# Stick-breaking attention layer: mask added at the scores, projections and output split into quarters and pairs between the head pairs

## The chip, the cores and the metric

One core of a Trainium2 chip runs the whole program, a stack of six stages in float32. The metric is the device time of one execution in microseconds. A core has five engines with an instruction stream each: TensorE (PE, matmuls into the accumulation memory PSUM), VectorE (DVE), ScalarE (ACT), GpSimd (POOL), and SyncE (SP), which here only issues transfers. They synchronize through semaphores.

## The reference, cut to what matters

The program computes conv mixer, experts, stick-breaking attention, experts, a state-space and dilated attention layer, and block attention, on 256 tokens of width 1024, with layer or RMS norms between. The change is in the third stage:

```python
z = jnp.einsum("bhqd,bhkd->bhqk", qb, kb) * scale
causal = s_idx < t_idx
log_keep = jnp.where(causal, jax.nn.log_sigmoid(-z), 0.0)
later = lax.cumsum(log_keep, axis=3, reverse=True) - log_keep
a = jnp.where(causal, jnp.exp(jax.nn.log_sigmoid(z) + later), 0.0)
outs.append(jnp.einsum("bhqk,bhkd->bhqd", a.astype(vb.dtype), vb))
...
return jnp.einsum("bse,ed->bsd", o, w_o)
```

16 heads of 64 columns; `x = layer_norm(ALPHA * x + mix)` follows. The expert stage behind it routes every token to 2 of 32 experts, and the kernel streams the weights of all 32.

## The kernel before, in words

Activations lie on 128 partitions, in two tiles of 128 tokens (`x[:, t]`), and transposed (`xT`). Weights come in chunks of 2 MB through a ring of six slots: SP's `load(g)` waits until chunk g - 6 has been used (`chunk_done`), then fills its slot. The stick-breaking stage has 8 chunks: q, k, v for heads 0 to 7 (chunks 0, 1, 2), the same for heads 8 to 15 (3, 4, 5), and the output matrix in two halves (6, 7). The first four-expert group of the next stage also loads four chunks outside the ring; the first of them waits until all chunks of the stage before are used (`sp.wait_ge(chunk_done, b0)`, L430). After that the expert weights stream without a stop.

PE's order in the stage (`stick_breaking`, L852 on): transposes of x, projection chunks 0 and 1 (`channels`, L587) and 2 (`tokens`, L597) whole, then ten turns of a loop over pairs of heads. Turn n issues `z(n+1)`, the transposed scores of pair n+1 (banks 0 and 1, 384 columns for each head, that is three 128x128 blocks); `fill()`, a half of projection chunk 3, 4 or 5 (L873, L878; eight or sixteen matmuls into bank 6 or 7) in the first five turns, two in turn 0; `later(n-1)`, the running sums over keys as matmuls with a triangular and an all-ones matrix (banks 2 and 3, L904 to L908); and `mix(n-2)`, weights times values (bank 4 or 5, L922, L925). In turns 8 and 9 the output of chunk 6 stands before `later` and `mix` (`output_tile`: residual as a matmul with ALPHA times the identity, L605, then L618, tile 0 in banks 0 and 1, tile 1 in banks 2 and 3), and chunk 7 comes after the loop. In this trace one fp32 matmul call appears as two instructions.

For each pair the other engines do a chain, each step released by a semaphore:

1. ACT copies the scores out of PSUM (`copy_z`, L1371) to `sk_z`.
2. DVE takes the magnitude of z (`magnitude`, L1917); ACT takes exp(-|z|) (L1382) and log(1 + that) (L1391); DVE adds max(z, 0) (`soft`, L1925), which gives softplus.
3. POOL multiplies it by the 0/1 mask `stick_mul` (L542).
4. PE: `later`. DVE: z minus the sums (`logs`, L1935), then minimum with 0 and the mask `stick_add` of 0 and -1e30 (L1938). ACT: exp (L1387). PE: `mix`. ACT: copy to `sk_mixT` (L1399), which the output reads.

Buffers `sk_z`, `sk_l`, `sk_sp`, `sk_a` are double. `take` (L1352) is ACT's copy of a finished projection chunk. The scores of the next pair need the banks of the last one (`sk_z`), `later` needs the banks 2 and 3 read by `logs` (`sk_d`). After tile 0's last output matmul (`tile_out`) DVE runs its layer norm (`statistics`, L1677, to `scaled`, L1695), and tile 1's after the last chunk.

Elsewhere, L1981 adds a mask to attention scores from PSUM, L2067 multiplies 512 columns of PSUM, L1957 scales 1024 columns in SBUF by a scalar, and L2127 is another one-source operation on 1024 columns.

## Time and profile before

| | us |
|---|---|
| three runs | 1782.76, 1782.93, 1788.47 |
| median | 1782.93 |
| profiled execution | 1790.54 |
| its span, first to last instruction | 1788.6 |
| PE busy in the span | 1617.0 (90%) |
| VectorE, ScalarE, GpSimd busy | 364.7, 272.4, 106.2 |
| mean granted TensorE clock | 0.977 |

The profile is one execution of the program. Its page gives the busy time of each engine, the span in slices and the chain of work that ended last; queries give groups of instructions by line, waits, stretches and timelines. "PEclk" is the TensorE clock granted in a stretch as a share of full speed, 2.4 GHz. The DMA share is that of the core's 16 DMA engines.

### The profile page before, as it was taken

How to read it: one execution, taken by the hardware profiler on the slowest of the kernel's cores; microseconds unless marked ns; L12 is line 12 of the kernel's file. 1: busy time of each engine (PE TensorE's matmuls, PEld its weight loads, DVE VectorE, ACT ScalarE, POOL GpSimd, SP SyncE). 2: the span in 40 equal slices, each digit the busy share in tenths (PEclk: the TensorE clock that was granted, in tenths of full speed). 3: DMA queues.
4: the chain of work that ended last, by engine and by line, in shares of the span. 5: the costliest groups of instructions: out<-in, count | busy, mean ns of one | idle time of the engine just before them, and what ended most of it. 6: DMA issues, size and time to landing. Idle time of an engine off the chain costs nothing.

```text
span 1788.6 us, 24177 instructions
## 1 busy us (share of the span) xinstructions
PE 1617.0 (90%) x10394; PEld 1002.2 (56%) x10394; DVE 364.7 (20%) x770; ACT 272.4 (15%) x651; POOL 106.2 (6%) x160
## 2 busy tenths in 40 slices
PE   8998999888998898889988898886999999989998
PEld 7855555555555665455555555554884444645553
DVE  1932000000000212240000000003234452330322
ACT  2011000000000113210000000001133322311331
POOL 0000000000000002100000000000001233003110
PEclk9999999999999899899999999997999999989998
DMA  9529999999999732179999999999242232233100
GB/s 402 220 99 424 427 427 429 428 429 429 428 429 428 317 141 94 41 328 426 427 429 428 429 429 428 428 428 403 95 147 113 75 137 95 94 141 141 48 1 24
DMA packets 36186, 504.61 MB, mean 282 GB/s; under 512 B 4000, under 2 KB 4128, under 8 KB 5792
## 3 DMA queue, kind: packets, MB, share of 16 engines
q1 hardware_dynamic: 34976, 499.59, 67.1%
q0 software_dynamic: 1152, 4.19, 0.6%
q8 instruction: 43, 0.70, 0.2%
q14 instruction: 15, 0.12, 0.0%
HBM read 502.72 MB, written 1.05 MB: 282 GB/s over the span
## 4 chain that ended last, share of the span: by engine, by line
PE 74%; DMA 18%; DVE 4%; ACT 2%; issue 1%; POOL 0%; SPq 0%; ACTq 0%; DVEq 0%
DMA ring<-in_expert_up 17%; PE ps L974 12%; PE ps L587 10%; PE ps L703 9%; PE ps L720 7%; PE ps L618 7%; PE ps L760 7%; PE ps L687 4%; PE ps L772 3%; PE ps L969 2%; PE ps L873 2%; PE ps L564 1%; PE ps L1028 1%; PE ps L878 1%; PE ps L597 1%
## 5 line engine op out<-in xcount | busy, mean ns | idle before, releaser
L703 PE MATMUL ps<-x_tok,constants_sb 128*128 128x256 f32 x1232 | 307.2, 392 | 0.0
L720 PE MATMUL ps<-ring,arena 128*32 128x256 f32 x3968 | 238.2, 382 | 53.0 <-DMA ring<-in_expert_up 50.0
L703 PEld LDWEIGHTS ps<-x_tok,constants_sb 128*128 128x128 f32 x1232 | 221.6, 190 | 104.9 <-issue 81.3
L974 PE MATMUL ps<-ring,spare 128*128 128x512 f32 x480 | 217.5, 607 | 0.8 <-DVE spare L1631 0.8
L720 PEld LDWEIGHTS ps<-ring,arena 128*32 128x32 f32 x3968 | 121.4, 110 | 160.3 <-DMA ring<-in_expert_up 41.2
L587 PE MATMUL ps<-spare,ring 128*128 128x256 f32 x832 | 184.6, 385 | 2.1 <-DMA ring<-in_stream 1.3
L587 PEld LDWEIGHTS ps<-spare,ring 128*128 128x128 f32 x832 | 160.7, 194 | 25.2 <-DVE spare L1628 2.9
L974 PEld LDWEIGHTS ps<-ring,spare 128*128 128x128 f32 x480 | 90.2, 193 | 111.7 <-issue 109.8
L618 PE MATMUL ps<-ring,arena 128*128 128x512 f32 x288 | 129.3, 606 | 2.4 <-DVE arena L2203 1.4
L760 PE MATMUL ps<-ring,arena 128*32 128x512 f32 x960 | 115.0, 598 | 13.3 <-ACT arena L1306 13.3
L1821 DVE TENSOR_TENSOR arena<-arena,ps 128x128 f32<-128x128 f32 x64 | 18.4, 288 | 518.0 <-ACT arena L1311 518.0
L618 PEld LDWEIGHTS ps<-ring,arena 128*128 128x128 f32 x288 | 55.1, 194 | 70.5 <-issue 65.7
L1311 ACT ACTIVATE arena<-ps 128x128 f32<-128x128 f32 x64 | 17.7, 277 | 471.6 <-PE ps L720 471.6
L772 PE MATMUL ps<-arena,root_w 128*128 128x512 f32 x128 | 59.2, 605 | 13.0 <-DVE arena L1826 13.0
L687 PE MATMUL ps<-arena,x_tok 128*128 128x128 f32 x576 | 69.0, 280 | 0.8 <-DVE arena L1790 0.8
L687 PEld LDWEIGHTS ps<-arena,x_tok 128*128 128x128 f32 x576 | 67.3, 196 | 1.1 <-DVE arena L1790 1.1
L760 PEld LDWEIGHTS ps<-ring,arena 128*32 128x32 f32 x960 | 27.0, 109 | 67.3 <-issue 67.3
L1826 DVE COPY arena<-ps 128x512 f32<-128x512 f32 x16 | 11.1, 692 | 234.5 <-PE ps L760 234.5
L772 PEld LDWEIGHTS ps<-arena,root_w 128*128 128x128 f32 x128 | 23.0, 190 | 50.5 <-DVE arena L1826 27.5
L495 POOL TENSOR_TENSOR spare<-spare 128x16 f32<-128x16 f32 x10 | 2.2, 220 | 807.8 <-ACT spare L1435 807.6
L1450 ACT ACTIVATE spare<-spare 128x128 f32<-128x128 f32 x80 | 35.4, 443 | 59.2 <-DVE spare L1990 59.2
L969 PE MATMUL ps<-spare,ring 128*128 128x256 f32 x192 | 42.7, 381 | 0.0
(269 smaller groups left out, 1257.8 us busy)
## 6 DMA issues: line engine op xcount, KB each, us to landing
ring<-in_expert_up SPq DMA_DIRECT2D x124, 2048.0 KB, 24.5
ring<-in_expert_down SPq DMA_DIRECT2D x60, 2048.0 KB, 27.1
ring<-in_stream SPq DMA_DIRECT2D x44, 2048.0 KB, 8.2
arena<-in_expert_up SPq DMA_DIRECT2D x4, 2048.0 KB, 14.4
arena<-in_expert_down SPq DMA_DIRECT2D x2, 2048.0 KB, 21.6
spare<-in_expert_down SPq DMA_DIRECT2D x2, 2048.0 KB, 18.0
constants_sb<-in_constants SPq DMA_DIRECT2D x1, 1766.0 KB, 17.7
x_tok<-in_x SPq DMA_DIRECT2D x1, 1024.0 KB, 5.1
```

The lines of the kernel that those rows point to most:

```text
L587: ins = pe.matmul(o, w[:, k, m * P:(m + 1) * P], xT[:, k, :], start=(k == 0), stop=(k == KT - 1))
L618: ins = pe.matmul(bank(2 * t + n), mixT[:, 4 * c + k, t * P:(t + 1) * P], w[:, k, n * 512:(n + 1) * 512], start=(scale is None and c == 0 ...
L687: ins = pe.matmul(ps[:, 6 + half, k * P:(k + 1) * P], x[:, t, kk * P:(kk + 1) * P], pick[:, t].rearrange("p e s -> p (e s)"), start=(t == ...
L703: pe.matmul(ps[:, b, 0:TOK], ident, x[:, 0, 0:TOK], start=True, stop=True, skip_group_check=True)
L720: ins = pe.matmul(ps[q * SLOTS:(q + 1) * SLOTS, 4 + e % 2, 0:TOK] .rearrange("p (g n) -> p g n", g=2), xg[:, 4 * half + k, e * SLOTS:(e + ...
L760: ins = pe.matmul(ps[e * SLOTS:(e + 1) * SLOTS, 6 + n, :], hidT[:, e, k * SLOTS:(k + 1) * SLOTS], w[:, e, n * 512:(n + 1) * 512], start=(k ...
L772: ins = pe.matmul(bank(2 * t + n), back[:, t * P:(t + 1) * P], yg[:, n * 512:(n + 1) * 512], start=False, stop=False, skip_group_check=True)
L873: ins = pe.matmul(ps[:, 6 + part, (m % 2) * TOK:(m % 2 + 1) * TOK], w[:, k, m * P:(m + 1) * P], xT[:, k, :], start=(k == 0), stop=(k == KT ...
L969: ins = pe.matmul(ps[:, b + part, (m % 2) * TOK:(m % 2 + 1) * TOK], w[:, k, m * P:(m + 1) * P], xT[:, k, :], start=(k == 0), stop=(k == KT ...
L974: ins = pe.matmul(bank(b + part), xT[:, k, part * P:(part + 1) * P], w[:, k, :], start=(k == 0), stop=(k == KT - 1))
L1450: act.activation(at_p[:, hh, c], at_sm[:, hh, c], ACT.Exp, bias=at_nmx[:, t, h:h + 1], accum_out=at_den[:, out_g, t, h:h + 1])\
L1821: dve.tensor_tensor(hid[:, e % 2, :], sg[:, e % 2, :], ps[:, 4 + e % 2, P:TOK], mul)\
```

## The change

The mask is added to the scores on DVE as they leave PSUM (`masked`), instead of ACT's plain copy; with -1e30 in a masked place, softplus is 0 and the last exponential is 0, so POOL's multiply and the mask in `logs` go, and with them the constant `stick_mul`. `logs` is now two subtractions and a minimum with 0. `later` writes its first 256 columns of both heads into bank 2 (as one 512-column matmul) and the last 128 of each head into the free columns 384 to 511 of the score banks 0 and 1, behind a wait until the next pair's scores have been masked. `mix` uses the two halves of bank 3. That frees banks 4 to 7: the output of tile 0 gathers in banks 6 and 7, that of tile 1 in 4 and 5 (`STICK_OUT`), and can begin before all pairs are done. The loop is written out by hand: projection chunks 3 to 5 in quarters (`quarter`) and the output by pair k and token tile t (`out(t, k)`, two matmuls) stand between the steps of the pairs. `mix(n)` now comes in the same round as `later(n)`, not one turn later.

```diff
 CONST, CONST_WORDS = layout([
-    ("mean", P), ("iota", SLOTS), ("rev8", 8), ("rev4", 4), ("stick_mul", HEAD_COLS),
+    ("mean", P), ("iota", SLOTS), ("rev8", 8), ("rev4", 4),
...
-                if stage == STICK:
-                    for pr in range(SB_PAIRS):
-                        sp = sk_sp[:, pr % 2]
-                        pool.wait_ge(sem("sk_sp"), pr + 1)
-                        pool.tensor_tensor(sp, sp, C("stick_mul").unsqueeze(1)
-                                           .broadcast_to([P, 2, HEAD_COLS]), ALU.mult)\
-                            .then_inc(sem("sk_spm"), 1)
...
+                def quarter(c, q):
+                    if q == 0:
                         pe.wait_ge(sem("sk_taken"), 2 if c == 3 else c)
                         arrive(pe, g + c)
                     w = slot8[slot(g + c)]
                     if c < 5:
+                        for k in range(KT):
+                            ins = pe.matmul(ps[:, 6 + q // 2, (q % 2) * TOK:(q % 2 + 1) * TOK],
+                                            w[:, k, q * P:(q + 1) * P], xT[:, k, :],
+                                            start=(k == 0), stop=(k == KT - 1))
                     else:
+                        t = q // 2
+                        for k in range(4 * (q % 2), 4 * (q % 2) + 4):
+                            ins = pe.matmul(bank(6 + t), xT[:, k, t * P:(t + 1) * P], w[:, k, :],
+                                            start=(k == 0), stop=(k == KT - 1))
+                    if q == 3:
                         ins.then_inc(chunk_done, 1)
+
+                def seed(t):
+                    pe.wait_ge(sem("sk_taken"), 6 if t == 0 else 3)
+                    for n in range(2):
+                        pe.matmul(bank(STICK_OUT[t] + n), C("alpha"),
+                                  x[:, t, n * 512:(n + 1) * 512], start=True, stop=False,
+                                  skip_group_check=True)
+
+                def out(t, k):
+                    c = k // 4
+                    arrive(pe, g + 6 + c)
+                    pe.wait_ge(sem("sk_oT"), k + 1)
+                    w = slot4[slot(g + 6 + c)]
+                    for n in range(2):
+                        ins = pe.matmul(bank(STICK_OUT[t] + n), sk_mixT[:, k, t * P:(t + 1) * P],
+                                        w[:, k % 4, n * 512:(n + 1) * 512], start=False,
+                                        stop=(k == KT - 1), skip_group_check=True)
+                    return ins
 
                 def z(pr):
                     if pr:
                         pe.wait_ge(sem("sk_z"), pr)
+                        pe.wait_ge(sem("sk_d"), 2 * (pr - 1))
...
                 def later(pr):
-                    pe.wait_ge(sem("sk_spm"), pr + 1)
+                    pe.wait_ge(sem("sk_sp"), pr + 1)
                     if pr:
-                        pe.wait_ge(sem("sk_d"), pr)
+                        pe.wait_ge(sem("sk_d"), 2 * pr)
+                    m, o = sk_sp[:, pr % 2], ps[:, 2, :].rearrange("p (h c) -> p h c", h=2)
+                    pe.matmul(o, C("from_on"), m[:, :, 0:TOK], start=True, stop=False,
+                              skip_group_check=True)
+                    pe.matmul(o[:, :, P:], ones, m[:, :, TOK:], start=False, stop=True,
+                              skip_group_check=True)
+                    pe.wait_ge(sem("sk_z"), min(pr + 2, SB_PAIRS))
                     for hh in range(2):
+                        ins = pe.matmul(ps[:, hh, HEAD_COLS:], C("from_on"), m[:, hh, TOK:],
+                                        start=True, stop=True)
...
-                    if pr >= 2:
-                        pe.wait_ge(sem("sk_oT"), pr - 1)
+                    if pr:
+                        pe.wait_ge(sem("sk_oT"), pr)
+                    c = (pr % 2) * TOK
...
+                            o = ps[64 * hh:64 * hh + 64, 3, c:c + TOK]
```

PE's order after the change, one round to a line (Q = quarter(chunk, q), O = out(t, k)):

```
channels(g), channels(g+1), tokens(g+2) tile 0, z(0), tokens tile 1
Q(3,0) z(1) later(0) Q(3,1) Q(3,2) mix(0)
Q(3,3) z(2) later(1) Q(4,0) Q(4,1) mix(1)
Q(4,2) z(3) later(2) Q(4,3) mix(2)
seed(1) O(1,0) z(4) later(3) Q(5,0) Q(5,1) mix(3)
Q(5,2) Q(5,3) z(5) later(4) O(1,1) O(1,2) mix(4)
O(1,3) z(6) later(5) seed(0) O(0,0) mix(5)
O(0,1) z(7) later(6) O(0,2) O(0,3)[chunk 6 done] mix(6)
O(0,4) later(7) O(0,5) O(0,6) mix(7)
O(1,4) O(0,7)[tile 0 out] O(1,5) O(1,6) O(1,7)[chunk 7 done]
```

ScalarE and VectorE:

```diff
-                    act.activation(sk_z[:, pr % 2], ps[:, 0:2, 0:HEAD_COLS], ACT.Copy)\
-                        .then_inc(sem("sk_z"), 1)
...
+                for n in range(SB_PAIRS):
+                    if n == 1:
+                        take(3)
+                    if n == 4:
+                        take(5)
+                    act.wait_ge(sem("sk_arg"), n + 1)
+                    act.activation(sk_a[:, n % 2], sk_a[:, n % 2], ACT.Exp)\
+                        .then_inc(sem("sk_a"), 1)
                     if n + 1 < SB_PAIRS:
+                        log_part(n + 1)
+                    if n == 2:
+                        take(4)
+                    act.wait_ge(sem("sk_o"), n + 1)
+                    c = (n % 2) * TOK
+                    act.activation(sk_mixT[:, n, :], ps[:, 3, c:c + TOK], ACT.Copy)\
+                        .then_inc(sem("sk_oT"), 1)
...
+                def masked(pr):
+                    dve.wait_ge(sem("sk_scored"), pr + 1)
+                    if pr >= 2:
+                        dve.wait_ge(sem("sk_d"), 2 * (pr - 1))
+                    dve.tensor_tensor(sk_z[:, pr % 2], ps[:, 0:2, 0:HEAD_COLS], later_mask, add)\
+                        .then_inc(sem("sk_z"), 1)
...
+                    dve.tensor_tensor(w[:, :, 0:TOK], z[:, :, 0:TOK],
+                                      ps[:, 2, :].rearrange("p (h c) -> p h c", h=2), sub)\
+                        .then_inc(sem("sk_d"), 1)
+                    dve.tensor_tensor(w[:, :, TOK:], z[:, :, TOK:], ps[:, 0:2, HEAD_COLS:], sub)\
+                        .then_inc(sem("sk_d"), 1)
+                    dve.wait_ge(sem("sk_d"), 2 * (pr + 1))
+                    dve.tensor_scalar(w, w, 0.0, None, ALU.min).then_inc(sem("sk_arg"), 1)
...
+                masked(0)
                 magnitude(0)
+                soft(0)
+                for n in range(SB_PAIRS):
+                    if n + 1 < SB_PAIRS:
+                        masked(n + 1)
+                    logs(n)
                     if n + 1 < SB_PAIRS:
                         magnitude(n + 1)
+                        soft(n + 1)
```

`log_part` holds the exponential and the logarithm that stood in the loop before. The layer norm reads the new banks.

## Rows read from the trace of the kernel before

**Rows 1.** Stretches: us, busy us (count) of PE PEld DVE ACT POOL, PEclk, DMA, GB/s:

```profile
597.49:769.47 171.98, 153.45 (x617) 103.82 (x618) 34.17 (x43) 35.32 (x48) 18.99 (x8) 0.94 0.31 116
640.93:769.47 128.54, 110.01 (x458) 72.09 (x458) 34.17 (x43) 33.27 (x46) 18.99 (x8) 0.93 0.23 82
670.00:680.00 10.00, 10.00 (x60) 8.68 (x56) 1.94 (x3) 2.51 (x3) 2.47 (x1) 1.00 0.17 34
705.00:733.00 28.00, 16.63 (x87) 12.61 (x87) 11.90 (x13) 11.71 (x16) 7.35 (x3) 0.78 0.17 68
770.03:1226.00 455.97, 406.68 (x3634) 245.49 (x3633) 38.56 (x113) 34.26 (x100) 1.12 (x2) 1.00 1.01 427
```

**Rows 2.** Waits between 597 and 772 us: total us, times, longest us:

```profile
PE ps L904 <- POOL arena L542: 9.1, 3, 4.0
...
PE ps L892 <- ACT arena L1371: 6.3, 5, 2.0
```

**Rows 3.** Timeline of SP's queue: start us, us, issues merged over the waits between:

```profile
754.38 15.61 SPq L414 DMA_DIRECT2D ring<-in_expert_up  x2
770.03 0.91 SPq L433 DMA_DIRECT2D arena<-in_expert_up  x2
```

**Rows 4.** Timeline of PE in the stage, matmuls of one line merged:

```profile
597.49 29.72 PE L587 MATMUL ps<-spare,ring 128*128 128x256 f32 x128 [0.78 <-DVE spare L1628]
...
640.87 0.71 PE L892 MATMUL ps<-arena 64*128 64x256 f32 x4
...
643.57 14.08 PE L873 MATMUL ps<-spare,ring 128*128 128x256 f32 x64
657.59 0.71 PE L892 MATMUL ps<-arena 64*128 64x256 f32 x4
...
669.65 0.71 PE L892 MATMUL ps<-arena 64*128 64x256 f32 x4 [1.95 <-ACT arena L1371]
...
670.51 7.17 PE L873 MATMUL ps<-spare,ring 128*128 128x256 f32 x32
...
742.53 0.60 PE L904 MATMUL ps<-arena,constants_sb 128*128 128x256 f32 x2
...
744.38 0.65 PE L922 MATMUL ps<-arena 128*64 128x256 f32 x4
...
745.49 1.99 PE L605 MATMUL ps<-x_tok,constants_sb 128*128 128x512 f32 x4 [0.25 <-DVE arena L1935]
...
755.63 14.00 PE L618 MATMUL ps<-ring,arena 128*128 128x512 f32 x32 [0.48 <-ACT arena L1399]
769.47 1.04 PE L564 MATMUL ps<-constants_sb,x_tok 128*128 128x128 f32 x8
```

**Rows 5.** VectorE's groups by line and shape, whole kernel: busy us, mean ns:

```profile
L1981 DVE TENSOR_TENSOR spare<-ps,constants_sb 128x768 f32<-128x768 f32 x20 | 19.1, 957 | 9.2 <-PE ps L1017 9.1
...
L1957 DVE TENSOR_SCALAR arena<-x_tok,small 128x1024 f32<-128x1024 f32 x4 | 2.8, 750 | 0.1
L2067 DVE TENSOR_TENSOR arena<-ps,arena 128x512 f32<-128x512 f32 x4 | 2.6, 686 | 21.9 <-PE ps L1093 21.9
```

**Rows 6.** Groups by line and shape between 597 and 770 us:

```profile
L542 POOL TENSOR_TENSOR arena<-arena,constants_sb 128x768 f32<-128x768 f32 x8 | 19.0, 2374 | 120.8 <-DVE arena L1925 120.8
...
L1391 ACT ACTIVATE arena<-arena,constants_sb 128x768 f32<-128x768 f32 x8 | 7.4, 923 | 0.1
...
L1387 ACT ACTIVATE arena<-arena 128x768 f32<-128x768 f32 x8 | 6.7, 843 | 1.1 <-DVE arena L1938 0.8
```

**Rows 7.** Timeline of VectorE at the stage's end:

```profile
762.80 1.29 DVE L1677 BATCH_NORM_STATS2 small<-ps 128x6 f32<-128x512 f32 x2 [16.37 <-PE ps L618]
...
769.67 1.30 DVE L1677 BATCH_NORM_STATS2 small<-ps 128x6 f32<-128x512 f32 x2 [1.86 <-PE ps L618]
```

**Rows 8.** Timeline of POOL and VectorE in a later stage: start us, us:

```profile
1440.02 2.04 POOL L504 TENSOR_TENSOR arena<-arena,spare 128x512 f32<-128x512 f32 x2
...
1441.31 1.30 DVE L2127 TENSOR_SCALAR arena<-arena 128x1024 f32<-128x1024 f32 x1
```

More of the change, by code:

```diff
@@ new lines, in stick_breaking @@
+                ins.then_inc(chunk_done, 1)
+                quarter(3, 0)
+                z(1)
+                later(0)
+                quarter(3, 1)
+                quarter(3, 2)
+                mix(0)
+                quarter(3, 3)
+                z(2)
+                later(1)
+                quarter(4, 0)
+                quarter(4, 1)
+                mix(1)
+                quarter(4, 2)
+                z(3)
+                later(2)
+                quarter(4, 3)
+                mix(2)
@@ new lines, in stick_breaking @@
+                seed(1)
+                out(1, 0)
+                z(4)
+                later(3)
+                quarter(5, 0)
+                quarter(5, 1)
+                mix(3)
+                quarter(5, 2)
+                quarter(5, 3)
+                z(5)
+                later(4)
+                out(1, 1)
+                out(1, 2)
+                mix(4)
+                out(1, 3)
+                z(6)
+                later(5)
+                seed(0)
+                out(0, 0)
@@ new lines, in stick_breaking @@
+                mix(5)
+                out(0, 1)
+                z(7)
+                later(6)
+                out(0, 2)
+                out(0, 3).then_inc(chunk_done, 1)
+                mix(6)
+                out(0, 4)
+                later(7)
+                out(0, 5)
+                out(0, 6)
+                mix(7)
+                out(1, 4)
+                out(0, 7).then_inc(tile_out, 1)
+                for k in (5, 6, 7):
+                    ins = out(1, k)
+                ins.then_inc(chunk_done, 1)
```

108 lines of the change are left out of this document (24 added, 84 removed).

## The prediction

> **What bounds the kernel now.** I read the table of stretches first. The stage that changes runs from the first projection matmul at 597.49 us to the first transpose of the next stage at 769.47 us, 171.98 us. In it TensorE (PE) is busy 153.45 us; from 640.93 us on, where the pairs of heads begin, it is busy 110.01 of 128.54 us, at a mean granted clock of 0.93 [rows 1]. So 18.5 us are idle, and part of the busy time is at the lower clock: in 705 to 733 us PE is busy 16.63 of 28 us and the granted clock is 0.78, a mean over time at its two levels, 1.2 and 2.4 GHz.
>
> The reader should then see who PE waits for. The waits of the stage give it: before the "later" matmuls (L904) 9.1 us in three waits, the longest 4.0, all on POOL's mask multiply (L542), and before the scores (L892) 6.3 us in five, on ScalarE's copy of the previous scores (L1371) [rows 2]. Together 15.4 of the 18.5 us. VectorE, ScalarE and POOL are each busy under 36 us of the 172, so none is short of time; what ends the idle time is one pair's chain of dependent steps, three of whose turns have nothing else for PE to do, once the six projection halves are used up and before the output begins.
>
> What follows the stage matters as much. From 770.03 to 1226 us the DMA engines run at share 1.01 and 427 GB/s: the second expert stage is bound by its weights [rows 1]. And SP, which issued a ring load at 754.38 us, issues the next only at the end of the same row, 754.38 + 15.61 = 769.99 us, when the last output matmul of this stage is done, and the loads beside the ring at 770.03 us, right behind it [rows 3]. So every microsecond by which the last output matmul comes earlier starts the saturated stretch earlier, and I pass the shift on at one to one.
>
> **The change, part by part.** *Work of PE.* I sum what PE must do in the new order at full clock, taking start-to-start times of the PE timeline [rows 4], since a matmul's own end is modelled.
> - Channels of the first two chunks and tokens of the third: 640.87 - 597.49 = 43.4 us, unchanged.
> - Twelve quarters: one is (657.59 - 643.57)/4 = 3.51 us; those of the last chunk have 8 instructions of 512 columns for 16 of 256, the same columns. 42.1 us.
> - Eight scores: 670.51 - 669.65 = 0.86 us each. 6.9 us.
> - Eight "later": 744.38 - 742.53 = 1.85 us. The new form has one matmul of 512 columns and one of 256 for four of half the width: the same columns, so 1.85 again. 14.8 us.
> - Eight mixes: 744.38 to 745.49 less 0.25 idle, 0.86 us. 6.9 us.
> - Sixteen outputs by pair and tile, two matmuls of 512 columns each: (769.47 - 755.63)/8 = 1.73 us. 27.7 us. The two seeds with the residual have the same shape: 3.5 us.
>
> Sum 145.3 us, so an unbroken PE would reach the end at 597.49 + 145.3 = 742.8 us, 26.7 us earlier. Cross-check: 18.5 idle plus the half-clock share of the 153.45 busy us, 153.45 - 145.3 = 8.1, also 26.6.
>
> *Does PE stay unbroken?* Let L be the end of "later" of pair n. The next mix needs: subtraction of 512 columns, 0.69 us; of 256 columns, 0.42 (an estimate, from 957 ns for 768 columns and 686 for 512); the minimum over 768; the exponential, 0.84 [rows 5, 6]. The minimum is a one-source VectorE operation in SBUF that the stage did not have. The nearest rows are 0.75 us for 128x1024 (L1957) [rows 5] and 1.30 us for the same shape (L2127) [rows 8]; scaled to 768 columns 0.60 and 0.97 us. I take 0.60: at 1441.31 us, where L2127 stands, POOL was in elementwise work (from 1440.02 us for 2.04 us), and in the new stage it has none; 0.97 stays as the other end. With 0.60 the smallest margin below is 0.4 us, with 0.97 it is 0.05; the sum is the same. The Trainium skill (SBUF — State Buffer, "Who interferes with whom") says that a VectorE instruction in a two-port mode and GpSimd block each other for a whole instruction. By that rule the pair of rows is explained, the new minimum is at 0.60 because POOL's multiply goes, and rival (b) below is the less likely; no run shown yet tests it with this shape.
>
> With four hand-offs of 0.04 us the mix is ready at L + 0.69 + 0.42 + 0.60 + 0.84 + 0.16 = L + 2.7. PE has at least two outputs or one quarter in between, 3.46 us. Covered by 0.8 us.
>
> The next "later" needs: the same 1.71 us of logs, the magnitude 0.96, exponential 0.84, logarithm 0.92, soft 0.96, and six hand-offs: L + 5.6. The shortest cover is ahead of the last one: two outputs, a mix, an output, 3 x 1.73 + 0.86 = 6.05. Covered by 0.4 us; the two rounds before it have a score more, 6.9. In the first four rounds quarters make it 8.7 us or more. Before, the same loop held POOL's 2.37 us as well [rows 6], and three turns had no cover.
>
> *The mask.* Added on VectorE as the scores leave PSUM: 0.96 us per pair, by the identical shape of L1981 [rows 5], in place of ScalarE's copy of the same columns. New wait: "later" holds its second half until the next pair's scores are masked. Queued behind it on PE is everything, but the first half is 3/4 of 1.85, 1.4 us, against 0.96 and a hand-off; cost 0 while VectorE is free, else its soft step ahead delays both. POOL: eight multiplies go, 19.0 us [rows 6]; nothing else in its queue waits.
>
> *Moved.* The projection chunks 3 and 4 finish 1 to 2 us later than before, and with them their ring loads; each 2 MB load has 20 us until the next, cost 0. Output chunk 6 is done before the seventh mix instead of just before SP's issue at 754.38, so its load still lands before the end. SP and POOL are passed by nothing else. ScalarE's copies of the head outputs to SBUF, of 256 columns and so under the 0.84 of 768, are each needed by PE 1.7 us or more later. The constants shrink by 196 KB, at 427 GB/s between 0 and 0.5 us at the start; I take 0, because VectorE needs them only long after they land.
>
> *The tail.* The first tile is now complete three outputs before the end, 5.2 us, before it was 6.7 us. Its normalization takes 769.67 - 1.86 - 762.80 = 5.0 us [rows 7], so VectorE is ready for the second tile at about the same moment as its matmuls. Cost 0, with a margin of 0.1 to 0.2 us; that was 1.86 us.
>
> For joints between some forty groups I allow 0.5 us. Gain 26.2 us. Against the profiled execution (1790.54 us, its span 1788.6) that is 1764.3; that execution lies 7.6 us above the median of the runs, and the difference applied to the median, 1782.93, gives **1756.7 us**.
>
> **Rivals.**
> *(a) Forecast*, gain 25 to 28 us. 0.82.
> *(b) The close pairs run late.* In rounds 4 to 7 PE has only outputs as cover, with margins of 0.4 to 1.3 us. Speaks for it: every step is a serial hand-off, and the unseen minimum and the mask wait both stand in it. Against: even with 0.97 for the minimum the sum is covered. If each of the four rounds loses 1.5 us, 6 us in all: 1762.7, range 1759 to 1768. 0.13.
> *(c) The shift is not passed on*, because the expert weights or the first router steps end the same way whatever PE does. Then about 1782.9. Against it stands SP's own wait for the last output matmul [rows 3]. 0.03.
> *(d) Slower: the clock falls between the pairs.* 101.9 us of the sum lie after the first three chunks. At a mean granted clock g they last 101.9/g; break-even with the present 128.5 us is g = 0.79, and 0.75 would give 135.9, 7.4 us more: 1790.3. For it: 0.78 in 705 to 733 us. Against: that stretch had three pauses of 9.1 us in all, up to 4.0 us long [rows 2], and in 670 to 680 us, with scores, a half chunk, "later" and mix in turn, PE was busy 10.00 us at 1.00 [rows 1]. The Trainium skill (TensorE: Matmul & The Clock Gate, "A second HAM failure mode: psum-queue depth-cycling") tells of a kernel whose small idle spells between groups made the clock fall and rise again and again; this trace agrees only for the long pauses. 0.02.
> That the change does not do what it says would be a wait left in place; the POOL wait goes with its instruction, so this is part of (b).
>
> **How the numbers follow.** The forecast is (a). The range reaches down for a sum priced 1 us too high and the spread of the runs shown (1782.76 to 1788.47), and up through most of (b): 1753 to 1766. A difference under about 0.3%, 5.3 us, cannot be told from none here. (a) and (b) are faster, 0.95; (c) same, 0.03; (d) slower, 0.02.
>
> **What would show it.** In the changed profile: PE busy 145 to 147 us of about 146 between the first projection and the next transposes; granted clock there 0.99 or more; idle before "later" and the scores under 1 us together; the minimum at 0.6 us; SP's four loads at about 743.8 us instead of 770.0; the expert stretch unchanged in length at 427 GB/s; all later stages shifted by the same amount. Idle before "later" released by VectorE in the last four rounds would be (b). An unchanged time of the first expert matmul after SP's loads shifted would be (c).

## The result and the profile after

The changed kernel took 1760.11 us (median of 4 runs, 1757.25 to 1761.93) against 1784.8 for the kernel before (4 runs, 1782.76 to 1788.47): ratio 0.9855, 95% interval 0.9835 to 0.9875 (the medians by themselves give 0.9862). Forecast was 1756.7 us in 1753 to 1766, a gain of 26.2 us; the medians differ by 24.7 us, and the interval of the ratio stands for 22 to 29 us. The profiled execution took 1759.92 us, its span 1758.1.

The stretches that answer to [rows 1], of the changed kernel (us, busy us and count of PE, PEld, DVE, ACT, POOL; then granted clock, DMA share, GB/s):

```profile
597.60:744.47 146.87, 146.87 (x585) 94.40 (x586) 39.74 (x59) 30.12 (x40) 0.00 (x0) 0.98 0.36 136
640.87:744.47 103.60, 103.60 (x423) 62.15 (x422) 36.86 (x56) 26.30 (x36) 0.00 (x0) 1.00 0.28 102
744.47:1216.55 472.08, 410.59 (x3646) 246.82 (x3644) 50.14 (x143) 38.99 (x110) 1.05 (x2) 0.99 1.00 426
1216.55:1758.10 541.55, 513.05 (x1994) 307.09 (x1994) 171.66 (x314) 139.44 (x342) 82.58 (x140) 0.98 0.26 98
```

and the last of them in the kernel before:

```profile
1241.20:1788.60 547.40, 518.94 (x1994) 309.77 (x1994) 171.66 (x314) 139.45 (x342) 82.57 (x140) 0.96 0.26 97
```

The reader should see four things. The stage lasts 146.87 us where it lasted 171.98, and PE is busy in all of it. After the first groups the granted clock is 1.00, where it was 0.93. The expert stretch behind it is 472.08 us long; the same stretch before, from the first transpose at 769.47 us to the first transpose after it at 1241.20, took 471.73. So the 25.1 us came through it to within 0.35 us. And the rest of the program, which the change doesn't touch, took 541.55 us against 547.40; that is why the two spans differ by 30.5 us and not by 25. The last section comes back to it.

The first projection group of the stage (128 instructions) took 30.53 us here to the start of the next group, at clock 0.91, and 29.55 before, at 0.94, with the same code. It differs by up to 1.5 us between profiles, so the stage is better compared from the end of that group: 142.4 us before (627.04 to 769.47), 116.3 after (628.13 to 744.47), 26.1 us less. Of these, 18.5 are idle time and 7.6 are PE's busy time for the same work at a higher clock.

PE's timeline around the closest rounds, the sixth and seventh pair, to the end of the stage:

```profile
597.60 30.70 PE L579 MATMUL ps<-spare,ring 128*128 128x256 f32 x128 [0.78 <-DVE spare L1678]
...
720.87 0.71 PE L895 MATMUL ps<-arena 64*128 64x256 f32 x4
...
721.73 1.12 PE L905 MATMUL ps<-arena,constants_sb 128*128 128x512 f32 x2
...
723.57 3.60 PE L880 MATMUL ps<-ring,arena 128*128 128x512 f32 x8
727.09 0.65 PE L926 MATMUL ps<-arena 128*64 128x256 f32 x4
...
727.89 1.98 PE L880 MATMUL ps<-ring,arena 128*128 128x512 f32 x4
729.72 1.02 PE L905 MATMUL ps<-arena,constants_sb 128*128 128x512 f32 x2
...
731.45 3.60 PE L880 MATMUL ps<-ring,arena 128*128 128x512 f32 x8
734.98 0.65 PE L926 MATMUL ps<-arena 128*64 128x256 f32 x4
...
735.78 8.85 PE L880 MATMUL ps<-ring,arena 128*128 128x512 f32 x20
744.47 1.04 PE L556 MATMUL ps<-constants_sb,x_tok 128*128 128x128 f32 x8
```

No line between the first and the last has a bracket with idle time. Scores (L895), "later" (L905), outputs (L880) in twos and mix (L926) follow each other at 0.86, 1.84, 1.76 each and 0.80 us, start to start; an output piece that stands alone takes 1.83. VectorE in the same rounds, and at the tail:

```profile
728.12 0.96 DVE L1985 SCALAR_TENSOR_TENSOR arena<-arena 128x768 f32<-128x768 f32 x1 [1.88 <-ACT arena L1428]
731.65 0.69 DVE L1995 TENSOR_TENSOR arena<-arena,ps 128x512 f32<-128x512 f32 x1 [2.57 <-PE ps L911]
732.25 0.42 DVE L1998 TENSOR_TENSOR arena<-arena,ps 128x256 f32<-128x256 f32 x1
732.71 0.56 DVE L2001 TENSOR_SCALAR arena<-arena 128x768 f32<-128x768 f32 x1
739.52 1.29 DVE L1728 BATCH_NORM_STATS2 small<-ps 128x6 f32<-128x512 f32 x2 [6.25 <-PE ps L880]
...
744.67 1.29 DVE L1728 BATCH_NORM_STATS2 small<-ps 128x6 f32<-128x512 f32 x2
```

Soft (L1985) of the last pair ends at 728.12 + 0.96 = 729.08 us, and "later" of that pair starts at 729.72: 0.6 us in hand, where [rows 4] to [rows 6] gave 0.4. The minimum (L2001) takes 0.56 us. The statistics of tile 0 start at 739.52, those of tile 1 at 744.67 without idle time, 0.2 us after the next stage's first transpose (the timeline before had 1.86 us of idle time there [rows 7]). SP issues the loads that waited at 745.03:

```profile
727.20 17.79 SPq L414 DMA_DIRECT2D ring<-in_expert_up  x2
745.03 0.91 SPq L433 DMA_DIRECT2D arena<-in_expert_up  x2
```

that is 25.0 us earlier than in [rows 3].

### The profile page after: what moved, and what is told of

It is laid out like the page before. It is cut to its first block, busy times and chain, and to the rows that moved or that the text cites. A ratio compares the mean times of both kernels' runs of the same rounds, so it can differ in the third digit from the quotient of the medians.

```text
span 1758.1 us, 24121 instructions
## 1 busy us (share of the span) xinstructions
PE 1604.0 (91%) x10362; PEld 989.8 (56%) x10362; DVE 370.2 (21%) x786; ACT 267.2 (15%) x643; POOL 87.2 (5%) x152
## 4 chain that ended last, share of the span: by engine, by line
PE 75%; DMA 18%; DVE 4%; ACT 2%; issue 1%; SPq 0%; ACTq 0%; DVEq 0%
DMA ring<-in_expert_up 17%; PE ps L1030 12%; PE ps L579 11%; PE ps L695 9%; PE ps L712 7%; PE ps L752 7%; PE ps L610 5%; PE ps L679 4%; PE ps L764 3%; PE ps L1025 2%; PE ps L880 2%; PE ps L856 2%; PE ps L556 1%; PE ps L1084 1%; PE ps L862 1%
## 5 line engine op out<-in xcount | busy, mean ns | idle before, releaser
L712 PE MATMUL ps<-ring,arena 128*32 128x256 f32 x3968 | 238.2, 382 | 53.6 <-DMA ring<-in_expert_up 50.6
L1030 PE MATMUL ps<-ring,spare 128*128 128x512 f32 x480 | 213.8, 598 | 0.8 <-DVE spare L1681 0.8
L712 PEld LDWEIGHTS ps<-ring,arena 128*32 128x32 f32 x3968 | 121.4, 109 | 161.1 <-DMA ring<-in_expert_up 41.8
L752 PE MATMUL ps<-ring,arena 128*32 128x512 f32 x960 | 115.0, 597 | 13.3 <-ACT arena L1362 13.3
L610 PE MATMUL ps<-ring,arena 128*128 128x512 f32 x224 | 99.7, 601 | 1.9 <-DVE arena L2266 1.4
L610 PEld LDWEIGHTS ps<-ring,arena 128*128 128x128 f32 x224 | 42.5, 193 | 54.0 <-issue 50.0
L679 PE MATMUL ps<-arena,x_tok 128*128 128x128 f32 x576 | 70.3, 282 | 0.8 <-DVE arena L1841 0.8
L679 PEld LDWEIGHTS ps<-arena,x_tok 128*128 128x128 f32 x576 | 68.6, 199 | 1.1 <-DVE arena L1841 1.1
## 6 DMA issues: line engine op xcount, KB each, us to landing
arena<-in_expert_up SPq DMA_DIRECT2D x4, 2048.0 KB, 14.6
arena<-in_expert_down SPq DMA_DIRECT2D x2, 2048.0 KB, 21.4
```

Of the source, the lines that this page charges most:

```text
L610: ins = pe.matmul(bank(2 * t + n), mixT[:, 4 * c + k, t * P:(t + 1) * P], w[:, k, n * 512:(n + 1) * 512], start=(scale is None and c == 0 ...
L679: ins = pe.matmul(ps[:, 6 + half, k * P:(k + 1) * P], x[:, t, kk * P:(kk + 1) * P], pick[:, t].rearrange("p e s -> p (e s)"), start=(t == ...
L712: ins = pe.matmul(ps[q * SLOTS:(q + 1) * SLOTS, 4 + e % 2, 0:TOK] .rearrange("p (g n) -> p g n", g=2), xg[:, 4 * half + k, e * SLOTS:(e + ...
L752: ins = pe.matmul(ps[e * SLOTS:(e + 1) * SLOTS, 6 + n, :], hidT[:, e, k * SLOTS:(k + 1) * SLOTS], w[:, e, n * 512:(n + 1) * 512], start=(k ...
L1030: ins = pe.matmul(bank(b + part), xT[:, k, part * P:(part + 1) * P], w[:, k, :], start=(k == 0), stop=(k == KT - 1))
```

## The experiments

Theory A: the gain is PE's order of work. The projections and outputs cover the pair's chain of dependent steps, so that PE never waits and keeps its clock; the mask at the scores only makes the chain short enough for that cover; the expert stage's transfers pass the gain on whole. Theory B: POOL's multiply was the cause, and its removal would have given most of the gain in the old order too. Stage means, in what follows, the time from the first projection matmul to the next stage's first transpose, and expert stretch the time from there to the transposes behind the experts. Since the first projection group varies, the stage from the end of that group is given too, called the pairs' part: 142.4 us before, 116.3 in both profiles of the changed kernel. Totals of different rounds are compared loosely: the median of the kernel before was 1784.8, 1786.6, 1786.4 and 1786.6 us in the four rounds.

### The mask alone, in the old order

```diff
# against the kernel before
-                        pool.tensor_tensor(sp, sp, C("stick_mul").unsqueeze(1)
...
-                    pe.wait_ge(sem("sk_spm"), pr + 1)
+                    pe.wait_ge(sem("sk_sp"), pr + 1)
...
-                    act.activation(sk_z[:, pr % 2], ps[:, 0:2, 0:HEAD_COLS], ACT.Copy)\
+                    dve.tensor_tensor(sk_z[:, pr % 2], ps[:, 0:2, 0:HEAD_COLS],
+                                      C("stick_add").unsqueeze(1)
+                                      .broadcast_to([P, 2, HEAD_COLS]), add)\
...
+                    if pr + 2 < SB_PAIRS:
+                        masked(pr + 2)
                     dve.wait_ge(sem("sk_d"), pr + 1)
+                    dve.tensor_scalar(w, w, 0.0, None, ALU.min).then_inc(sem("sk_arg"), 1)
```

> The kernel before with one part of the change: the mask is added to the scores on VectorE, POOL's multiply and ScalarE's copy go, the minimum stands alone; PE's order of work stays as it was. Theory A (the gain is mostly the order of PE's work, and the mask only shortens a chain that is uncovered in three turns): in those three turns the 9.1 us of waits on POOL go, the minimum is 0.36 us shorter and the mask 0.15 us longer than the copy; what is late next is VectorE's row of four operations, about 3.5 us after each 'later', so some 1.8 us per turn stay idle. Stage 8 to 13 us shorter than before, 1775 us in all, ratio 0.994. Theory B (the POOL step was the cause of the stall and of the low clock, the new order adds little): 20 us or more, ratio 0.989 or below.

Measured: 1773.21 us (ratio 0.9934, 0.9909 to 0.9959), stage 162.17 us, 9.8 less than before. The pairs' part is 131.5 us, 11.0 less. The stage, and PE's waits in it:

```profile
597.37:759.54 162.17, 148.88 (x616) 100.86 (x617) 38.06 (x51) 29.70 (x40) 0.00 (x0) 0.97 0.33 123
```

```profile
PE ps L884 <- DVE arena L1915: 7.7, 6, 2.1
PE ps L896 <- DVE arena L1907: 2.8, 3, 2.0
...
PE ps L914 <- ACT arena L1371: 1.8, 3, 0.6
```

The multiply's 9.1 us have gone, and 13.3 us of idle time remain, 12.3 of them in these rows and most on VectorE: 7.7 before the scores (L884) on the mask, 2.8 before "later" (L896) on soft. A wait that goes leaves the next step of the same chain. The stage is as much shorter as expected, but not by the reasoning given: idle time fell by 5.2 us only (18.5 to 13.3), and the other 5.7 us of the 11.0 are PE's busy time, at a higher clock: 0.99 from the first pair on, with no pause over 2.1 us, against 0.93 with pauses of 2.6, 2.6 and 4.0 us. So theory B is right in one point: with POOL's step out of the chain most of the clock comes back even in the old order. The mask's step gives 11.0 of the 26.1 us, two fifths; the new order gives the other 15.1.

### POOL's multiply back in the new order

```diff
# against the changed kernel
+                        pool.tensor_tensor(sp, sp, C("stick_mul").unsqueeze(1)
+                                           .broadcast_to([P, 2, HEAD_COLS]), ALU.mult)\
+                            .then_inc(sem("sk_spm"), 1)
...
-                    pe.wait_ge(sem("sk_sp"), pr + 1)
+                    pe.wait_ge(sem("sk_spm"), pr + 1)
```

> The changed kernel with POOL's multiply by the 0/1 mask put back between soft and 'later' (it changes no value, the places are 0 already). Theory A: from one 'later' to the next the chain is 5.6 + 2.5 = 8.1 us; the cover is 6.9 us ahead of 'later' 5 and 6 and 6.05 ahead of 7, so about 1.2, 1.2 and 2.1 us of idle time on POOL, 4.5 us in all, none in the other rounds (least cover 8.7): 4 to 6 us above the changed kernel, ratio to before 0.988 to 0.989. Theory B: at least 10 us above it, most of the gain lost. The minimum stays at 0.56 us, since POOL's multiply does not fall in the same microseconds.

Measured: 1763.74 us (ratio 0.9882, 0.9857 to 0.9908), stage 147.79 us, pairs' part 118.4, 2.1 above the changed kernel. The total is 3.6 us above it where 4 to 6 were expected, a difference within the scatter of the runs; the waits are clearly smaller than expected: 0.28, 0.28 and 1.13 us, 1.7 and not 4.5, in the three rounds named and in no other:

```profile
712.00 1.13 PE L913 MATMUL ps<-arena,constants_sb 128*128 128x512 f32 x2 [0.28 <-POOL arena L542]
...
721.29 1.12 PE L913 MATMUL ps<-arena,constants_sb 128*128 128x512 f32 x2 [0.28 <-POOL arena L542]
...
730.57 1.12 PE L913 MATMUL ps<-arena,constants_sb 128*128 128x512 f32 x2 [1.13 <-POOL arena L542]
```

The multiply was mis-sized. Here it takes 1.81 us, not 2.45 (columns: minimum, median, maximum in ns, first and last start):

```profile
L542 POOL TENSOR_TENSOR arena<-arena,constants_sb x8: 1800/1806/1810, 639.8 to 728.7; 128x768 f32<-128x768 f32 x8
```

In the kernel before, seven of its eight calls took 2.45 us and the last 1.80: there VectorE's magnitude of the next pair, an operation on two SBUF inputs, ran beside all but the last. In the new order magnitude is done before soft. That takes 0.64 us off the multiply for each pair but the last. So of the 26.1 us of the pairs' part the new order with the mask at the scores gives 24.0 even with POOL's multiply in the chain, and taking the multiply out of it 2.1. (By the whole stage it would be 0.9, but this profile's first projection group was 1.2 us shorter, 29.36 us to the next group.) In the old order the mask's step gave 11.0. Theory B falls as an account of the gain; the parts depend on the order in which they are made, because they take away the same idle time.

### Nothing between the last pairs

```diff
# against the changed kernel
-                seed(1)
-                out(1, 0)
                 z(4)
...
                 z(5)
                 later(4)
-                out(1, 1)
-                out(1, 2)
                 mix(4)
...
                 later(7)
                 mix(7)
+                seed(1)
+                seed(0)
+                for k in range(4):
+                    out(1, k)
...
```

> The changed kernel with the sixteen output pieces and the two seeds moved behind the last mix; quarters, masks and chains as in the changed kernel. Theory A: from 'later' 4 on nothing covers the chain; 3.9 us idle ahead of 'later' 5 and 6, 4.7 ahead of 7, 2.7 ahead of the last mix, 15 us in all at full clock, and the granted clock falls below 1.00 there, some microseconds more: 15 to 21 us above the changed kernel, ratio to before 0.994 to 0.998. Theory B: under 8 us above it.

Measured: 1781.43 us (10 runs; ratio 0.9970, 0.9956 to 0.9984), 21.3 us above the changed kernel, just over the range expected; stage 167.66 us, 20.8 more; pairs' part 137.0, 20.7 more. Its waits, and the stage as one stretch:

```profile
PE ps L926 <- ACT arena L1437: 10.3, 4, 2.6
PE ps L905 <- DVE arena L1981: 3.1, 2, 2.0
...
PE ps L895 <- ACT arena L1414: 1.2, 1, 1.2
```

```profile
599.46:767.12 167.66, 153.13 (x584) 98.50 (x585) 39.62 (x59) 30.01 (x40) 0.00 (x0) 0.93 0.31 119
703.00:734.00 31.00, 17.62 (x89) 11.09 (x86) 14.57 (x21) 10.30 (x15) 0.00 (x0) 0.80 0.18 68
```

14.6 us are waits, 15 were expected; four times the mix (L926) waits 2.58 us for its exponential, which is the chain's first half (2.7 by the forecast's sum). The other 6 us are the clock: 0.93 over the stage, where the kernel before had 0.94. In the changed kernel these same matmuls run at 1.00. The output pieces as cover are worth 20.7 us in the new order, 14.5 of idle time and 6.1 of the clock that goes with it. That is more than the 15.1 us that separate the old order with the mask from the changed kernel, since the old order already has outputs of chunk 6 before its last "later" and its last mix. What the quarters of the projections are worth, against the halves of before, was not tested: they stand in every run in the new order.

### Ten microseconds more on PE

```diff
# against the changed kernel, ahead of seed(1)
+                for n in range(12):
+                    pe.matmul(bank(4 + n % 2), C("alpha"),
+                              x[:, 1, (n % 2) * 512:(n % 2 + 1) * 512], start=True, stop=True,
+                              skip_group_check=True)
```

> The changed kernel with twelve further matmul calls (24 instructions of 512 columns, 0.432 us each) ahead of the seed of tile 1, into banks 4 and 5, which the seed overwrites: 10.4 us of PE work. If the end of this stage sets the start of the saturated transfers, as forecast, the whole kernel is 10.4 us longer than the changed one (9.5 to 11.5), ratio to before 0.991, and the stretch from the first extra load to the end of the expert stage keeps its length. If the weights' transfers or the router set the end (rival c), the time hardly moves.

Measured: 1770.68 us (ratio 0.9919, 0.9890 to 0.9949), 10.6 us above the changed kernel, where the runs of each kernel spread over 5 to 6 us. The stage and the expert stretch:

```profile
599.60:755.47 155.87, 155.87 (x608) 98.04 (x609) 39.72 (x59) 30.14 (x40) 0.00 (x0) 0.99 0.34 128
755.47:1227.55 472.08, 412.29 (x3646) 248.02 (x3644) 50.12 (x143) 39.04 (x110) 1.05 (x2) 0.99 1.00 426
```

The stage is 9.0 us longer, with a first group of 29.24 us against 30.53; the pairs' part is 126.6, 10.3 longer, for 10.4 of added work. The expert stretch is 472.08 us, as in the changed kernel to the hundredth. The end of the stage sets the start of the saturated transfers, and the delay is passed on whole; rival (c) falls.

### The tail: yardstick and two variants

The changed kernel again, beside the next two on one chip:

> The changed kernel itself, beside the next two on one chip, as their yardstick: 1757 to 1762 us, ratio to before 0.985 to 0.987; stage 146 to 147 us.

Measured: 1762.19 us (1756.96 to 1764.51; ratio 0.9857, 0.9837 to 0.9877), stage 147.09 us (pairs' part 116.3), expert stretch 471.93. From the end of the first projection group to the end of the experts it is 588.3 us, and 588.4 in the first profile: a yardstick good to some 0.2 us.

Tile 0 completed later:

```diff
                 out(1, 4)
+                out(1, 5)
+                out(1, 6)
                 out(0, 7).then_inc(tile_out, 1)
-                for k in (5, 6, 7):
-                    ins = out(1, k)
-                ins.then_inc(chunk_done, 1)
+                out(1, 7).then_inc(chunk_done, 1)
```

> The changed kernel with the last output piece of tile 0 moved behind two more of tile 1: one output, 1.73 us, covers the normalization of tile 0 (5.0 us) instead of three. TensorE's stage is unchanged (146 to 147 us), the second tile's normalization and the router start 3.4 us later after it. The transfers go on from the same moment; the expert stretch gets 3.4 us longer less what they have in hand (1 to 1.5 us): 2 to 3.4 us above the changed kernel. If the margin of this tail were of no account, no difference.

Measured: 1763.25 us (ratio 0.9873, 0.9855 to 0.9891), by itself not to be told from the yardstick's. The trace tells more: from the first projection to the end of the expert stretch 622.08 us against 618.95 in the changed kernel's first profile, 3.1 more; from the end of the first group 592.7 against 588.4, 4.3 more, and so above the 2 to 3.4 expected. SP issues its next ring load 28.4 us after the loads that waited for the last output (743.64 and 772.01), where the changed kernel takes 22.8, and the transfers have run dry before it (right-hand columns: granted clock, DMA share, GB/s):

```profile
769.00:771.00 2.00, 2.00 (x30) 1.53 (x32) 0.64 (x3) 0.60 (x1) 0.00 (x0) 1.00 0.26 98
771.00:773.00 2.00, 2.00 (x44) 1.20 (x40) 0.24 (x1) 0.00 (x0) 0.00 (x0) 1.00 0.14 33
773.00:775.00 2.00, 2.00 (x44) 1.17 (x36) 0.29 (x1) 0.28 (x1) 0.00 (x0) 1.00 0.77 205
```

In the changed kernel the same issue comes at 767.86 us, and the same stretches stand at shares 0.98 to 1.04. The 5.5 us more between the issues are over the 3.4 of the work moved: the router's first 16 matmuls (L781) also took 3.56 us at clock 0.50, where they take 1.87 at 1.00 in the changed kernel.

The residual on VectorE for both tiles:

```diff
+                    if stage == STICK:
+                        step.run(dve.scalar_tensor_tensor(xt, xt, float(ALPHA), two_banks(at[t]),
+                                                          mul, add))
...
-                                        w[:, k % 4, n * 512:(n + 1) * 512], start=False,
+                                        w[:, k % 4, n * 512:(n + 1) * 512], start=(k == 0),
```

> The changed kernel without the two seeds on TensorE: VectorE adds ALPHA times x to the output as it leaves PSUM, and takes the statistics and the centring from SBUF. If the stage is bound by TensorE's work alone, as the changed kernel's trace says, it is 3.5 us shorter (143.4). The tail is dearer: the first tile's normalization is 1.27 us longer (6.3 against the 5.2 us that its three last outputs cover) and so is the second's, so the router ends 2.4 us later after the last output matmul, and the first ring slot of the expert stage is reused that much later. If the transfers have 1 to 1.5 us in hand there, 1 us comes back: 2 to 3.5 us less than the changed kernel in all. If they have none, 1 us less. Rival: the expert stretch takes the whole 2.4 us and more, no difference or slower.

Measured: 1759.52 us (ratio 0.9851, 0.9836 to 0.9867), not to be told from the changed kernel's. In the trace the last output ends 143.3 us after the first projection, as expected, but by luck: the first group was 1.2 us shorter than in the changed kernel's profile, and the stage is not bound by TensorE's work alone any more. Without the seed of tile 0 a single output stands between "later" and the mix of the sixth pair, and PE waits for its exponential:

```profile
714.53 0.65 PE L922 MATMUL ps<-arena 128*64 128x256 f32 x4 [0.86 <-ACT arena L1437]
```

From the end of the first group to the last output it is 114.0 us, 2.4 less than in the changed kernel, not 3.5. Then the first transpose waits 0.54 us, and the expert stretch takes 474.34 us. SP issues its next ring load 27.4 us after the loads that waited for the last output (741.41 and 768.79; 22.8 us in the changed kernel, 745.03 and 767.86), and the transfers run dry:

```profile
741.41 0.91 SPq L433 DMA_DIRECT2D arena<-in_expert_up  x2
...
768.79 2.05 SPq L414 DMA_DIRECT2D ring<-in_expert_down  x2
```

```profile
767.00:769.00 2.00, 2.00 (x43) 1.19 (x39) 0.85 (x2) 0.50 (x1) 0.00 (x0) 1.00 0.08 25
769.00:771.00 2.00, 2.00 (x44) 1.23 (x40) 0.16 (x1) 0.28 (x1) 0.00 (x0) 1.00 0.76 156
```

Nothing is kept: from the end of the first group to the end of the experts it is 588.9 us, against 588.4 and 588.3 (the 0.8 us that the whole, 618.19 against 618.95, seems to keep are the first group's). The expectation of 2 to 3.5 was too high for two reasons: the wait of 0.86 us inside the stage, and a router that came 4.6 us later after the last output, not 2.4. Up to the first expert's matmuls (L712), which start 25.8 us after the last output where the changed kernel's start 21.4 after it, the delay divides into 2.1 us of longer waits and 2.3 us of matmuls at a lower clock: the router's first 16 took 3.56 us at 0.50 (746.54 to 750.10), against 1.87 at 1.00.

The residual on VectorE for tile 1 alone:

```diff
-                    for n in range(2):
+                    for n in range(2 if t == 0 else 0):
...
+                                        start=(t == 1 and k == 0),
...
+                    if stage == STICK and t == 1:
+                        step.run(dve.scalar_tensor_tensor(xt, xt, float(ALPHA), two_banks(at[t]),
+                                                          mul, add))
```

> The changed kernel with one of the two seeds gone: the residual of tile 1 alone is added by VectorE, that of tile 0 stays on TensorE. The stage is one seed shorter, 1.73 us. Tile 0's normalization keeps its 5.0 us under three outputs, so the router ends only 1.25 us later after the last output matmul. The traces show how much the transfers have in hand there: in the kernel with both seeds gone they run dry 26 us after that matmul, and the changed kernel's next issue comes 23.4 us after it with about 1 us to its first bytes, so about 2 us. 1.25 fits under it: no dry spell, expert stretch 472 us as before, and the whole 1.7 us is kept, against 0.8 us of 3.6 in the kernel with both gone. Rival: the dry spell begins at any delay, and nothing is gained.

Measured: 1758.0 us (5 runs, 1757.25 to 1759.12; ratio 0.9840, 0.9823 to 0.9856), the lowest of all, though its interval overlaps the changed kernel's. The stage is 145.21 us (147.09 and 146.87 in the two profiles of the changed kernel), the pairs' part 114.6, 1.7 less, the expert stretch 471.74:

```profile
599.34:744.55 145.21, 145.21 (x580) 93.71 (x581) 39.73 (x59) 30.12 (x40) 0.00 (x0) 0.98 0.36 137
744.55:1216.29 471.74, 410.36 (x3646) 246.33 (x3644) 51.42 (x144) 38.99 (x110) 1.04 (x2) 0.99 1.00 426
769.00:771.00 2.00, 2.00 (x44) 1.22 (x40) 0.00 (x0) 0.23 (x1) 0.00 (x0) 1.00 0.99 418
```

From the end of the first group to the end of the experts it is 586.4 us, 1.9 to 2.1 less. PE waits nowhere in the stage: the seed of tile 0, which covers the sixth pair's mix, is still there. SP's issue comes 23.9 us after the waiting loads, and no stretch is dry. That it comes only 1.1 us later is partly luck: the router's first 16 matmuls lost 1.3 us at a lower clock here too, and the 32 matmuls ahead of the first expert's (L679) gained 1.5 at a higher one than in the changed kernel's profile. This version beats both kernels by the trace; by the totals it surely beats the one before, and the changed one probably.

### POOL busy beside the minimum

```diff
# against the changed kernel, on POOL, for each pair
+                        pool.wait_ge(sem("sk_later"), pr + 1)
+                        pool.tensor_tensor(sk_junk, C("att_add")[:, 0:2 * HEAD_COLS],
+                                           C("att_add")[:, 2 * HEAD_COLS:], ALU.add)\
+                            .then_inc(sem("sk_junked"), 1)
...
# on PE, ahead of the last three outputs
+                pe.wait_ge(sem("sk_junked"), SB_PAIRS)
```

> The changed kernel with an idle-running POOL addition of 768 columns (two SBUF inputs, into words that nothing reads) started at the end of each 'later', so that it runs beside the two subtractions and the minimum. If POOL's work beside it makes the minimum longer, as rows 8 had it, the minimum takes 0.8 to 1.4 us instead of 0.56, the mix and the next 'later' come that much later, and 'later' of pair 7, which has 0.6 us in hand, waits 0 to 0.5 us: total under 1.5 us more. If it does not, the minimum stays at 0.56 us and nothing moves.

Measured: 1763.2 us (2 runs; ratio 0.9868, 0.9842 to 0.9894), stage 147.27 us. One pair, and the group over the eight (mean ns behind the comma):

```profile
707.28 0.69 DVE L2003 TENSOR_TENSOR arena<-arena,ps 128x512 f32<-128x512 f32 x1 [0.95 <-PE ps L918]
707.39 1.81 POOL L541 TENSOR_TENSOR arena<-constants_sb 128x768 f32<-128x768 f32 x1 [15.72 <-PE ps L918]
...
708.34 1.29 DVE L2009 TENSOR_SCALAR arena<-arena 128x768 f32<-128x768 f32 x1
```

```profile
L2009 DVE TENSOR_SCALAR arena<-arena 128x768 f32<-128x768 f32 x8 | 10.2, 1278 | 0.3
...
L2003 DVE TENSOR_TENSOR arena<-arena,ps 128x512 f32<-128x512 f32 x8 | 5.5, 688 | 8.8 <-PE ps L918 8.8
L2006 DVE TENSOR_TENSOR arena<-arena,ps 128x256 f32<-128x256 f32 x8 | 3.3, 414 | 0.0
```

The minimum (L2009) takes 1278 ns in place of 560; it ends at 709.63, about 0.4 us after POOL's addition (709.20), while the subtractions beside it, which read one operand from PSUM, keep their 0.69 and 0.41 us. PE waits nowhere: the 0.7 us were in hand, where up to 0.5 us of waits was expected. So POOL's company lengthens a one-source minimum of this shape, which makes it the likely reason for the longer of the two rows that the forecast weighed; that row itself (L2127, one call) was not tested.

The Trainium skill (SBUF — State Buffer, "Who interferes with whom") says that a VectorE instruction in a two-port mode and GpSimd block each other, and that one with at most one SBUF input, outside the two-port modes, does not contend. By that rule this trace agrees, with 560 against 1278 ns for the one and 0.69 and 0.41 us unchanged for the other; no row names the mode of an instruction.

## Why the prediction was right, step by step

- *The sum of PE's work*, 145.3 us and a start-to-start time for each unit: right. The stage took 146.87 us, of which 1.0 is the clock of the first group (30.70 us in place of 29.72), so 0.6 us went to joints, forecast 0.5. From the end of the first group, which the clock changed in both profiles, the gain is 26.1 us against 26.2 forecast. Units: quarter 3.51 us, up to 3.65 where one stands alone; scores 0.86; "later" 1.84; mix 0.80 with an output behind it (0.86 forecast); output 1.74 in the last row of five, 1.83 to 1.92 where one stands alone. The forecast's cross-check of this sum was none: 18.5 + (153.45 - 145.3) is 171.98 - 145.3 written in another way, and called the 8.1 the clock's share without a row for it. The traces do show that share, 7.6 us of busy time.
- *An unbroken PE*: right; no wait, clock 1.00 from 640.87 us on. The forecast's sign of a granted clock of 0.99 or more over the stage was missed, 0.98, because of the first group alone. In hand were 0.6 us at the last "later", forecast 0.4. The chain was sized well (L + 5.5 measured from the end of "later" at 723.57 to soft's end at 729.08, forecast L + 5.6 with the hand-off), and even an added 0.7 us on the minimum did not break it.
- *The minimum at 0.60 us*: 0.56. But one reason was wrong. "The new minimum is at 0.60 because POOL's multiply goes": with the multiply back it is 560 ns as well, because the multiply stands 5 us away from it in the chain. It is POOL at work in the same microseconds that matters, as the last experiment shows.
- *The mask on VectorE at 0.96 us, its wait inside "later" free*: right, 958 ns; PE shows no idle time before the second half.
- *POOL's multiply priced at 2.37 us in the chain*: mis-sized for the new order, where it would be 1.81. It entered no term of the sum, only the expectation of the second experiment.
- *The tail at cost 0*: right. Tile 0's normalization ended with no idle time before tile 1's. The transfers had about 2 us in hand there that the forecast did not know of: the next ring load was issued 22.8 us after the loads that waited in the changed kernel, 24.6 us in the first and fourth experiments, without a loss (472.0 and 472.1 us of expert stretch), while 27.4 and 28.4 us left the transfers dry.
- *Passed on one to one*: right, 471.7 to 472.1 us for the expert stretch in nine profiles whose stages lasted 145.2 to 171.98 us. The two others, with a delayed tail, took 473.5 and 474.3.
- *The number*: 1756.7 forecast, 1760.11 measured. The stage's own gain was forecast 26.2 and was 25.1, the missing 1.1 being the first group's clock and 0.1 of joints. The other 2.3 us of the difference lie in the measurement: the median of the kernel before was 1782.93 in three runs and 1784.8 in four, and the changed one's was 1760.11 and 1762.19 in two sets. So (a) held. (b) did not come; the second experiment, with 1.8 us more in the chain, shows that even then three rounds lose 1.7 us together, where (b) had 6. (c) is refuted by the fourth. (d) is not what this change did: without pauses the clock stayed up, and where pauses of 2.58 us were put back it fell to a mean of 0.93 (third experiment). With the level of four runs, 1784.8, the same gain would have given 1758.6 us.

## What to carry to other kernels

When several engines are each mostly idle, sum what the bound engine has to do at full speed and compare it with the stage: the difference is what order alone can give, and here work that was there already, cut to pieces of 1.7 to 3.5 us and laid between dependent steps, gave 15.1 us with the chain already short, while shortening the chain gave 11.0 us in the old order and its last step (POOL's multiply) only 2.1 in the new. Count the lower clock as a cost of pauses beside their own length: it was 7.6 of the 26.1 us. Count the cover round by round against the chain, since the shortest round decides, and count it again after every piece taken away: two seeds less gave nothing, one less 2 us. Before two profiles are compared, find a stretch with the same code in both and see how much it differs by itself; here 1.2 us of it would have turned a multiply's 2.1 us into 0.9 and a loss of half a microsecond into a gain of 0.8. And look at what the stage's end starts: where saturated transfers wait for it, the gain is passed on whole, but the first steps behind it must issue the next transfer before the queued ones run out.

## What the runs showed of the hardware

The clock explains much of the scatter between profiles. The same first projection group of the stage, 128 instructions behind the same pause of 0.78 us, took 29.40 to 29.72 us in five profiles (the one before and the second, fourth, both-seeds-gone and late-tile-0 experiments) and 30.70 to 30.92 in the six others. In the last stage a group of 96 instructions behind a pause of 0.78 us took 43.46 us in the kernel before and 41.47 in the changed one:

```profile
1604.10 43.46 PE L974 MATMUL ps<-ring,spare 128*128 128x512 f32 x96 [0.78 <-DVE spare L1631]
```

```profile
1577.26 41.47 PE L1030 MATMUL ps<-ring,spare 128*128 128x512 f32 x96 [0.78 <-DVE spare L1681]
```

Which of the two lengths comes is not set by the code: the changed kernel's own second profile has 43.41 us for this group. In its first 4 us the granted clock was 0.50 in the kernel before, 1.00 in the changed one and 0.51 in that second profile. Behind the expert stage the changed profile was 5.9 us shorter with the same 1994 instructions and the same idle time (28.5 us in both); all of it is PE's busy time, 518.94 against 513.05 us, at mean clocks of 0.96 and 0.98. The second profile of the changed kernel has 515.95. That is more than many a change is worth, and a difference of two spans is therefore read stage by stage.

What a pause does to the clock varied too. Behind pauses of 2.56, 2.55 and 3.97 us in the kernel before, the next 3 to 5 us had mean clocks of 0.52, 0.61 and 0.50. In the third experiment the mix behind the first of four pauses of 2.58 us ran at 0.50, and those behind the second and third, just as long, at full clock. With no pause over 2.11 us among the pairs in the first experiment, the stretch from 700 to 735 us stayed at 1.00, though PE was idle for 6.5 us of it.

The second surprise is the price of POOL's neighbour on both sides: its multiply 2.45 us beside VectorE's two-operand operation in SBUF and 1.81 without, and VectorE's minimum 1.28 us beside POOL's addition and 0.56 without.
